# Two transformer blocks on one core: bias rows in parts, other PSUM banks for layer 1's latent tiles, and the place of a query rotation

## What is computed

```python
h = rmsnorm(x, ln_mix_g[l])
proj = h @ w_in[l]     # 1024 x 4128: qa, ka, va | qb, kb, vb | cq (768), ckv (256), kr (32)
ya = dilated_window_attention(qa, ka, va, bias_table[:, :8])   # A: 8 heads, relative bias
yb = differential_attention(qb.., kb.., vb, lam, bias_b)       # B: 4 heads, relative bias
qc = rmsnorm(cq, g) @ w_uq[l]      # 8 heads x (64 + 32); the last 32 columns are rotated
kvc = rmsnorm(ckv, g) @ w_ukv[l]   # C: keys and values; kr is rotated and shared
yc = mla_attention(...)
gates = sigmoid(h @ w_gate[l] + b_gate[l])
x = x + (gates0 * (ya @ w_br_a) + gates1 * (yb @ w_br_b) + gates2 * (yc @ w_br_c)) @ w_o
x = x + (silu(h2 @ w_ffn_gate) * (h2 @ w_ffn_up)) @ w_ffn_down
```

## Time and profile before

| | us |
|---|---|
| median of 3 runs | 1823.41 |
| lowest and highest | 1823.18, 1825.93 |
| the profiled execution's own time | 1823.75 |
| its span | 1822.0 |
| mean granted TensorE clock | 0.996 |

### The profile page before, as it was taken

How to read it: one execution, slowest core, us unless ns; L and a number is a source line. 1 busy time by engine, 2 the same in 40 slices (tenths; PEclk the granted TensorE clock), 3 DMA queues, 4 the chain that set the end, 5 groups by cost and what they waited for, 6 DMA issues and landing times.

```text
span 1822.0 us, 27283 instructions
## 1 busy us (share of the span) xinstructions
PE 1758.1 (96%) x9254; PEld 1451.1 (80%) x9254; DVE 1275.3 (70%) x1973; ACT 890.5 (49%) x1530; POOL 54.8 (3%) x111
## 2 busy tenths in 40 slices
PE   8999999998999999999999999999999999999998
PEld 3776778996766789988898877788789989778886
DVE  5788897667788885568547887555555579865555
ACT  1456334443455444444556664444445557544443
POOL 0000010000000000001000000000000000000000
PEclk9999999999999999999999999999999999999999
DMA  8866568764765566653665434555546644345553
GB/s 299 266 214 220 163 219 298 254 229 138 256 219 197 196 210 209 209 188 115 204 217 155 135 121 150 185 182 187 177 145 201 208 129 159 117 151 185 185 186 125
DMA packets 215955, 346.22 MB, mean 190 GB/s; under 512 B 19531, under 2 KB 113273, under 8 KB 215593
## 3 DMA queue, kind: packets, MB, share of 16 engines
q1 hardware_dynamic: 213368, 338.89, 57.7%
q0 software_dynamic: 1632, 5.39, 0.9%
q10 hardware_dynamic: 850, 0.54, 0.1%
HBM read 343.69 MB, written 1.07 MB: 189 GB/s over the span
## 4 chain that ended last, share of the span: by engine, by line
issue 80%; PE 12%; DVE 4%; DVEq 1%; POOLq 1%; POOL 1%; ACT 0%; DMA 0%; SPq 0%; ACTq 0%
PE acc L150 2%; PE acc L148 2%; PE acc L149 2%; PE prod L223 1%; PE prod L225 1%; PE prod L224 1%; DVE w_lo L134 1%; DVEq L937 1%; PE prod L148 1%; DVE proj L938 1%; PE prod L149 1%; PE prod L150 1%; PE turn L262 0%; DVE x_res L938 0%; DVE x_res L936 0%
## 5 line engine op out<-in xcount | busy, mean ns | idle before, releaser
L134 DVE TENSOR_TENSOR w_lo<-w_raw,w_hi 128x1024 fp32r<-128x1024 f32 (+2 forms) x584 | 643.4, 1122 | 313.5 <-ACT w_hi L128 307.9
L128 ACT CAST w_hi<-w_raw 128x1024 fp32r<-128x1024 f32 (+2 forms) x584 | 557.8, 968 | 410.0 <-PE acc L150 181.6
L148 PE MATMUL prod<-w_hi,hT_hi 128*128 128x344 f32 (+2 forms) x912 | 330.5, 362 | 5.6 <-ACT proj_b L1946 5.5
L150 PE MATMUL prod<-w_hi,hT_lo 128*128 128x344 f32 (+2 forms) x912 | 323.2, 354 | 0.0
L149 PE MATMUL prod<-w_lo,hT_hi 128*128 128x344 f32 (+2 forms) x912 | 322.4, 354 | 0.0
L148 PEld LDWEIGHTS prod<-w_hi,hT_hi 128*128 128x128 f32 x912 | 172.3, 189 | 27.8 <-DVE gates L2200 4.8
L150 PEld LDWEIGHTS prod<-w_hi,hT_lo 128*128 128x128 f32 x912 | 172.2, 189 | 15.4
L149 PEld LDWEIGHTS prod<-w_lo,hT_hi 128*128 128x128 f32 x912 | 172.7, 189 | 14.5
L223 PE MATMUL prod<-uT_hi,w_hi 128*128 128x256 f32 x448 | 127.1, 284 | 1.4 <-DVE w_lo L134 0.9
L148 PE MATMUL prod<-w_hi,uT_hi 128*128 128x512 f32 x304 | 124.6, 410 | 2.7 <-DVE uT_lo L301 1.3
L224 PE MATMUL prod<-uT_lo,w_hi 128*128 128x256 f32 x448 | 126.4, 282 | 0.0
(11 more groups left out here) (349 smaller groups left out, 2785.4 us busy)
## 6 DMA issues: line engine op xcount, KB each, us to landing
w_raw<-in_w_in_dram SPq DMA_DIRECT2D x72, 512.0 KB, 3.9
ada_raw<-in_w_ada_dram SPq DMA_DIRECT2D x68, 512.0 KB, 6.8
w_raw<-in_w_in_dram SPq DMA_DIRECT2D x192, 172.0 KB, 2.4
w_raw<-in_w_up_dram SPq DMA_DIRECT2D x64, 512.0 KB, 4.3
w_raw<-in_w_down_dram SPq DMA_DIRECT2D x64, 512.0 KB, 4.7
w_raw<-in_w_gate_dram SPq DMA_DIRECT2D x128, 192.0 KB, 2.7
w_raw<-in_w_ffn_gate_dram SPq DMA_DIRECT2D x88, 256.0 KB, 3.5
w_raw<-in_w_ffn_up_dram SPq DMA_DIRECT2D x88, 256.0 KB, 4.2
```

The source lines that it names most:

```text
L128: act.copy(self.hi[:, s, 0:cols], self.raw[:, s, 0:cols]).then_inc(self.hi_done, 1)
L134: dve.tensor_tensor(self.lo[:, s, 0:cols], self.raw[:, s, 0:cols], self.hi[:, s, 0:cols].bitcast(F32), ALU.subtract).then_inc(self.lo_done, 1)
L148: pe.matmul(out, a_hi, w_hi, start=first and c == 0, stop=False)
L150: mm = pe.matmul(out, a_lo, w_hi, start=False, stop=last and c == chunks - 1)
```

## The change

Six edits, in the second block only. SP, layer 0: the one load of the bias rows becomes six of two heads each (`BIAS_PARTS`), part b in front of the weights of tile 5 + b; the eight small loads now come first. PE reverses pair b behind tile 5 + b, when part b is in. ACT copies pairs 1, 3, 5 behind its steps 2, 4, 6, DVE pairs 0, 2, 4 likewise, and the rotation of the key columns stands behind DVE's copy of pair 0. Layer 1's tiles 0 to 3 go round `first_banks` as layer 0's do, and ACT casts tile 1's four groups before it waits for the row scale. `rope_q` moves into the last `branch_a`, behind one of its three low parts. The loops over input tiles on SP, ACT, DVE (from tile 7) and PE become straight code.

```diff
+BIAS_PARTS = (AH + BH) // 2
...
-                    sp.dma_start(bias_flipped, bass.AP(tensor=scratch.tensor, offset=0,
-                                                       ap=[[1, P], [REL, AH + BH], [1, SEQ]])).then_inc(bias_in, 16)
...
-                with sp.Fori(1, IN2_T - LAT_TILES) as t:
-                    in_tile(t, Pos(4 * LAT_TILES, (l, G2), (t, 4)))
+                for t in range(1, IN2_T - LAT_TILES):
+                    if l == 0 and t <= BIAS_PARTS:
+                        b = t - 1
+                        sp.dma_start(bias_flipped[:, 2 * b:2 * b + 2, :],
+                                     bass.AP(tensor=scratch.tensor, offset=2 * b * REL, ap=[[1, P], [REL, 2], [1, SEQ]])).then_inc(bias_in, 16)
+                    in_tile(t, layer(l, 4 * (LAT_TILES + t), G2))
...
                     for tok in range(TOKS):
                         square_x(2 * l, tok)
+                    split(layer(l, 4, G2), 4, KG * IN2_W)
                 act.wait_ge(x_rstd_done, layer(l, TOKS - 1, 2 * TOKS).count(1))
...
-                    with act.Fori(0, LAT_TILES) as t:
-                        split(Pos(4, (l, G2), (t, 4)), 3, KG * IN2_W)
-                        take_scaled(Pos(0, (l, N2), (t, 1)), Pos(3, (l, G2), (t, 4)), in_cols(t + (IN2_T - LAT_TILES)), IN2_W)
-                        split(Pos(7, (l, G2), (t, 4)), 1, KG * IN2_W)
+                    for t in range(LAT_TILES):
+                        if t > 0:
+                            split(layer(l, 4 + 4 * t, G2), 3, KG * IN2_W)
+                        take_scaled(layer(l, t, N2), layer(l, 3 + 4 * t, G2), in_cols(t + (IN2_T - LAT_TILES)), IN2_W, first_banks[t])
+                        if t > 0:
+                            split(layer(l, 7 + 4 * t, G2), 1, KG * IN2_W)
...
-                if l == 0:
-                    for b in (1, 3):
-                        take_bias(act.copy, act, b)
...
-                if l == 0:
-                    take_bias(act.copy, act, 5)
-                with act.Fori(2, IN2_T - LAT_TILES - 1) as t:
-                    in_step(t, Pos(4 + 4 * LAT_TILES, (l, G2), (t, 4)), Pos(LAT_TILES, (l, N2), (t, 1)))
+                for t in range(1, IN2_T - LAT_TILES - 1):
+                    in_step(t, layer(l, 4 + 4 * (LAT_TILES + t), G2), layer(l, LAT_TILES + t, N2))
+                    if l == 0 and t % 2 == 0:
+                        take_bias(act.copy, act, t - 1)
...
-                if l == 0:
-                    for b in (0, 2):
-                        take_bias(dve.tensor_copy, dve, b)
...
-                split(layer(l, 9 + 4 * LAT_TILES, G2), 2, KG * IN2_W)
-                rope(dve, proj[:, :, KR:], cos, sin, ROPE // 2, rope_tmp_k)
-                split(layer(l, 11 + 4 * LAT_TILES, G2), 1, KG * IN2_W)
-                if l == 0:
-                    take_bias(dve.tensor_copy, dve, 4)
-                with dve.Fori(2, IN2_T - LAT_TILES - 1) as t:
-                    split(Pos(4 + 4 * LAT_TILES, (l, G2), (t, 4)), 4, KG * IN2_W)
+                split(layer(l, 9 + 4 * LAT_TILES, G2), 3, KG * IN2_W)
+                for t in range(2, IN2_T - LAT_TILES - 1):
+                    split(layer(l, 4 + 4 * (LAT_TILES + t), G2), 4, KG * IN2_W)
+                    if l == 0 and t % 2 == 0:
+                        take_bias(dve.tensor_copy, dve, t - 2)
+                    if t == 2:
+                        rope(dve, proj[:, :, KR:], cos, sin, ROPE // 2, rope_tmp_k)
...
-                    split(nxt, 3, KG * GW)
+                    if last:
+                        split(nxt, 1, KG * GW)
+                        for tok in range(TOKS):
+                            taken_tiles(dve, tok, layer(l, N2_UKV + 1, N2), 2)
+                        rope_q()
+                        split(nxt + 1, 2, KG * GW)
+                    else:
+                        split(nxt, 3, KG * GW)
...
-                for tok in range(TOKS):
-                    taken_tiles(dve, tok, layer(l, N2_UKV + 1, N2), 2)
-                rope_q()
...
-                    with pe.Fori(1, LAT_TILES) as t:
-                        tile(Pos(0, (l, G2), (t, 4)), Pos(0, (l, N2), (t, 1)), uT, 0, 4, IN2_W)
...
+                for t in range(1, LAT_TILES):
+                    banks = [bank[:, 0:IN2_W] for bank in first_banks[t]]
+                    for g in range(4):
+                        W.multiply(pe, layer(l, 4 * t + g, G2), uT, KG * g, IN2_W, KG, banks, g == 0, g == 3,
+                                   vacant=vacated(layer(l, 1, N2)) if t == 3 and g == 0 else None)
+                for t in range(LAT_TILES, IN2_T - 1):
+                    tile(layer(l, 4 * t, G2), layer(l, t, N2), uT, 0, 4, IN2_W)
+                    b = t - LAT_TILES - 1
+                    if l == 0 and 0 <= b < BIAS_PARTS:
+                        if b == 0:
+                            pe.wait_ge(consts_in, 16 * 2)
+                            for tok in range(TOKS):
+                                taken_tiles(pe, tok, layer(l, 2, N2), 2)
+                        reverse_bias(b)
```

More of the change, by code:

```diff
@@ L2027, in scalar @@
                 sq.then_inc(lat_sq_done, 1)
-                in_step(1, layer(l, 8 + 4 * LAT_TILES, G2), layer(l, LAT_TILES + 1, N2))
-                if l == 0:
-                    take_bias(act.copy, act, 5)
-                with act.Fori(2, IN2_T - LAT_TILES - 1) as t:
-                    in_step(t, Pos(4 + 4 * LAT_TILES, (l, G2), (t, 4)), Pos(LAT_TILES, (l, N2), (t, 1)))
+                for t in range(1, IN2_T - LAT_TILES - 1):
+                    in_step(t, layer(l, 4 + 4 * (LAT_TILES + t), G2), layer(l, LAT_TILES + t, N2))
+                    if l == 0 and t % 2 == 0:
+                        take_bias(act.copy, act, t - 1)
                 for tok in range(TOKS):
@@ L2543, in qk_turns, with reverse_bias @@
                     T.turn(pe, fill + x, [(P, slice(tok * P, (tok + 1) * P), rows[:, tok, x, :]) for tok in range(TOKS)])
-            def reverse_bias(banks):
-                for b in banks:
-                    if b >= 4:
-                        pe.wait_ge(bias_out, 4)
-                    for h in range(2):
-                        mm = pe.matmul(acc[b % 4][:, h * SEQ:(h + 1) * SEQ], flip, bias_flipped[:, 2 * b + h, :], start=True, stop=True)
-                    mm.then_inc(bias_turned, 1)
+            def reverse_bias(b):
+                pe.wait_ge(bias_in, 16 * (b + 1))
+                if b >= 4:
+                    pe.wait_ge(bias_out, 4)
+                for h in range(2):
+                    mm = pe.matmul(acc[b % 4][:, h * SEQ:(h + 1) * SEQ], flip, bias_flipped[:, 2 * b + h, :], start=True, stop=True)
+                mm.then_inc(bias_turned, 1)
             for l in range(LAYERS):
@@ L2565, in tensor @@
                                   lambda n, k: T.awake(pe, layer(l, n, F2), k), 3, 3, h_halved)
-                    for t in range(1, LAT_TILES):
-                        banks = [bank[:, 0:IN2_W] for bank in first_banks[t]]
-                        for g in range(4):
-                            W.multiply(pe, layer(l, 4 * t + g, G2), uT, KG * g, IN2_W, KG, banks, g == 0, g == 3,
-                                       vacant=vacated(layer(l, 1, N2)) if t == 3 and g == 0 else None)
                 else:
@@ L2572, in tensor @@
                     turned_tile(layer(l, 0, G2), IN2_W, outs(IN2_W), h_turn, h_taken, h_halved, vacated(layer(l, 0, N2)))
-                    with pe.Fori(1, LAT_TILES) as t:
-                        tile(Pos(0, (l, G2), (t, 4)), Pos(0, (l, N2), (t, 1)), uT, 0, 4, IN2_W)
-                tile(layer(l, 4 * LAT_TILES, G2), layer(l, LAT_TILES, N2), uT, 0, 4, IN2_W)
-                if l == 0:
-                    pe.wait_ge(consts_in, 16 * 2)
-                    pe.wait_ge(bias_in, 16)
-                    for tok in range(TOKS):
-                        taken_tiles(pe, tok, layer(l, 2, N2), 2)
-                    reverse_bias(range(4))
@@ L2582, in tensor @@
-                tile(layer(l, 4 * LAT_TILES + 4, G2), layer(l, LAT_TILES + 1, N2), uT, 0, 4, IN2_W)
-                if l == 0:
-                    reverse_bias(range(4, 6))
-                with pe.Fori(LAT_TILES + 2, IN2_T - 1) as t:
-                    tile(Pos(0, (l, G2), (t, 4)), Pos(0, (l, N2), (t, 1)), uT, 0, 4, IN2_W)
+                for t in range(1, LAT_TILES):
[3 more added lines that the diff above has]
+                                   vacant=vacated(layer(l, 1, N2)) if t == 3 and g == 0 else None)
```

## The result

The changed kernel takes 1813.3 us (median of five runs, 1811.6 to 1816.3) against 1823.4 for the kernel before; the ratio is 0.9938, with a 95% interval of 0.9927 to 0.9949. The profiled execution took 1815.4 us, its span is 1813.6 us. The forecast was 1813.6 us (1814.0 for the profiled execution, with a span near 1812.2). The sum came out; one of its four terms did not, and others made up for it.

What follows compares the result with a forecast made beforehand. TensorE (PE), busy 96% of the span, was taken as the bound. Gains of 4.1 + 0.55 + 2.1 + 3.0 = 9.75, taken as 9.8 us, off 1823.41 gave 1813.6 us, range 1810.8 to 1817.6.

Steps and rivals of the forecast that it cites:

- the prediction's own signs: Profile signs named beforehand, among them PE's gap before layer 0's tile 5 under 2 us and clock 1.00 behind it.
- Part A: Layer 0's input product: bias rows loaded in six parts shorten the wait before tile 5 and keep the clock; gain 4.1 us.
- the latents' 0.55: PE's wait just behind layer 0's input product, from weights queued behind the gate bias, taken as gained: 0.55 us.
- would be cast at 874.20: Layer 0, tile 5's weights: issued at 870.33, cast at 874.20 before 0.4 us for the part's own traffic.
- rival 1: Tile 5's weights stay late because broadcasts hold the queue; PE waits 3 us, the clock falls: 1817.0 us, chance 0.12.
- Part B: Layer 1's input product: alternate banks let tile 1 start without waiting for ACT to empty tile 0's; gain 2.1 us.
- Part C: Last pair of branch A, both layers: moving branch C's query rotation removes PE's 2.42 us wait; gain 1.5 us a layer.
- Loops: Loops to straight code on PE, ACT, DVE and SP: priced at nothing, bound 1.4 us.
- Rival 2: The rotation is only moved: the next gate tile waits as long as the turn did; 1816.6 us, chance 0.09.
- Rival 3: Gains are given back downstream, since DVE's and DMA's pace sets branches A to C; 1820.4 us, chance 0.05.
- Rivals 4 and 5: Slower: straight code must be fetched, 1831.8 us, chance 0.02; cycling banks costs layer 1's clock, 1833.8 us, chance 0.01.
- 8.9 us for one transfer of 1.5 MB: Estimate from the skill's DMA table for the whole bias load, set against 12 us for six 256 KB parts.

Runs made afterwards that it cites:

- spread: Changed kernel with layer 0's six small vector loads issued one each behind the weights of tiles 5 to 10, lambda computed later; 1806.6 us.
- vec_early: Changed kernel with layer 0's eight vector loads issued ahead of tile 4's weights; 1812.0 us.
- without_c: Changed kernel with the rotation of branch C's queries back ahead of the last pair, in both layers; 1818.5 us.
- lat_early: Changed kernel with layer 0's two latent gains issued ahead of tile 4's weights, the six small loads left in place; 1810.2 us.
- part_behind2: Changed kernel with each of the six bias parts issued behind its tile's weights, each with its own semaphore; 1812.7 us.
- vec_pool2: Changed kernel with layer 0's eight vector loads issued by POOL on its own queue; 1812.5 us.
- pe_loop: Changed kernel with PE's tiles 4 to 10 of layer 1 in a hardware loop again; 1814.2 us.
- small_early: Changed kernel with layer 0's six small loads issued ahead of tile 4's weights, the two latent gains left in place; 1809.8 us.

## Why the prediction came out, point by point

The number came out by luck: the largest term failed, and terms taken too low or at nothing made up for it. By the prediction's own signs (under 2 us of wait ahead of tile 5, clock 1.00 behind it) it was wrong there: the wait is 3.60 us, the clock 0.50.

**Part A, gain 4.1, and the latents' 0.55: wrong.** The issue time was right to 0.2 us. The failed step is the next one, "would be cast at 874.20", which carried layer 1's 3.87 us from issue to cast over to layer 0. Even without the six small loads it is 6.1 us in layer 0 (870.85 - 864.71), with them 7.3. The traces suggest that it depends on what was issued in a row just before. In spread that is the tables, 512 KB of gains and the part. In vec_early SP had paused from 865.5 to 867.5 behind the tables and the part, and the same weights took 2.4 us to land. How much of the 6.1 us each of these loads causes wasn't tried. So PE waited 3.60 us in place of 0.8, and the clock stayed at half for 18 matmuls, 886.28 - 880.96 = 5.32 us, where at full rate they take 18 x 0.16 + 0.1 = 3.0: 2.3 us lost in place of none. Those two make 5.1 us, about the whole of the term. The reversals cost 0.8 to 0.9 us each (tiles 8.44 us apart, 899.57 - 891.13, against 48 x 0.158 = 7.58), and the wait ahead of the latents did go. The forecast's rival 1 named this mechanism, broadcasts ahead of the weights, at 1817.0 and 0.12, and it is in the main what happened; the time that it gave was missed only because the terms below were too small. And the share that the forecast gave to the 1.5 MB load belongs to the six small loads: with them spread, the old order has 0.56 us of wait left.

That S1 as a whole is no longer than before (+0.25 us) isn't this part's doing alone. In layer 0 the straight code also takes 0.13 us off each of the tiles 7 to 10, some 0.5 us (see the loops below).

**Part B, 2.1: right.** The trace has tile 1 right behind tile 0, and undoing the part costs 2.0 us in its stretch.

**Part C, 1.5 for each layer: mechanism right, mis-sized.** The rotation fills the idle time and the gate bias comes at the forecast moment; 1.84 us in S2, 2.84 in S4. In S4 the clock had been at half behind the old wait: from the turn to the gate tile it took 8.70 us there and 7.08 in layer 0, 1.6 us more. Those came back too, less some 0.7 of waits on the gate bias: 0.69 us here for 0.42 there, and a new one of 0.40 at the branch products. That last one is not part C's, for without_c has it too (0.39); what made it wasn't looked for. The failed size is the clock behind the turn, which the forecast put at nothing: it read the clock behind two of its three waits and not behind this one, though the row that shows it (the turn of 1.11 us) lies in the same trace.

**Loops, nothing: mis-sized.** Of S3's 4.48 us, 2.1 are B and 1.0 the wait ahead of the query product (1.53 to 0.56, the landing of weights). Some 1.4 are left. They lie at the starts of the tiles. In the loops of the kernel before, tiles are 7.70 us apart in either layer (1395.49 and 1403.19 in layer 1), and 7.57 in straight code. That is 0.13 us at most of the tile starts, 1.1 in all, and 0.2 more is one wait on ACT that is gone. PE's loop over tiles 4 to 10 alone brings back 0.03 us a tile, 0.2 in all; the rest must lie with the other loops (PE's over tiles 1 to 3, ACT's, DVE's, SP's), which were not tried one by one. The Trainium skill, "Advanced Engine Details and Errata", Control Flow Timing, gives about 108 ns for a compare-and-branch; PE's loop alone shows less than a third of that for a tile, 0.03 us.

**Rivals 2 to 5.** None happened as a whole. Rival 2: 0.42 and 0.69 us came back at the gate tile, not 2.4. Rival 3: S5 is the same within 0.2 us, and beyond the waits on the gate bias no gain was given back. Rivals 4 and 5: no stall on straight code, and layer 1's cycling tiles ran at 0.16 a matmul.

**The sum.** Forecast 4.65 + 2.1 + 3.0 = 9.8; the trace, by stage, -0.25 + 1.84 + 4.48 + 2.84 - 0.18 = 8.7, and 8.4 in the span. The forecast was within 0.3 us of the median with half of its working replaced. In the working, 8.9 us for one transfer of 1.5 MB isn't interpolated: it carries the slope between the entries for 64 KB and 1 MB beyond 1 MB. No term of the sum uses it.

## What to carry to other kernels

Time from issue to use is a property of the queue at that moment: take it from a place where as much was issued just before, not from the same code in a later layer. When a wait ends on a transfer, look at the DMA rate in one or two microsecond windows before it; a trough with idle engines pointed at small loads ahead here, and these did best one at a time behind large ones, with their use moved back. And behind each wait that an edit removes, read the clock too.

## What the runs showed of the hardware that was not expected

Six loads that copy one short row of DRAM to all 128 partitions (193 KB together) leave SP's hardware queue at 40 to 60 GB/s with the DMA engines busy 0.2 of the time for about 4 us (lat_early, 866 to 870); the two gains, 512 KB in rows of 3 and 1 KB in place of 512 bytes and less, leave no such trough (302 GB/s). Layer 1 of the changed kernel has the trough as well (0.22 busy, 58 GB/s in 1360 to 1362), and there no wait of PE follows. On POOL's queue the same loads keep the engines busy (0.88) at 47 GB/s. The DMA view of 870 to 873 in the changed kernel counts what travelled:

```profile
DMA packets 550, 0.18 MB, mean 59 GB/s; under 512 B 474, under 2 KB 547, under 8 KB 550
```

So 474 of 550 packets are under 512 bytes. The Trainium skill, "DMA: Bandwidth & Descriptors", Specifications, asks for at least 512 B for line rate; the runs agree with it on the rate. Why the engines stand idle meanwhile on one queue and not on the other wasn't settled.

A wait of PE of 2.4 us is followed by half clock sometimes: in the kernel before in layer 1 and not in layer 0, in without_c in both. One of 2.85 us left the clock alone in part_behind2 and not in vec_pool2. One of 2.00 us did so in the kernel before (layer 1's tile 1) and not in pe_loop, and 1.81 and 2.08 us were followed by half clock in small_early and lat_early. In these runs the length of the wait alone doesn't decide it. The price, when it comes, was 1.2 us behind tile 5 in the kernel before, 1.6 in pe_loop and 2.3 in the changed kernel, and the S1 of vec_pool2 and part_behind2, with 2.85 us of wait each, differ by 3.0 us (109.91 - 106.95).
